# Two transformer blocks on one core: the first modulation as vector pieces, squares and means added on VectorE, activation tables loaded ahead

## What is computed

```python
# first block, layer 0 (mixer: latent attention, 8 heads), layer 1 (gated linear attention)
m_lat = (silu_c @ ada_w[i] + ada_b[i])      # 6 x 1024 values; m_ctx with silu_cc
h = modulate(rms_norm(x, norm_g[i, 0]), m[0], m[1])
x = x + m[2] * rms_norm(mixer(h), norm_g[i, 1])
h = modulate(rms_norm(x, norm_g[i, 2]), m[3], m[4])
x = x + m[5] * rms_norm(sqrelu_mlp(h, w1, w2), norm_g[i, 3])
# latent attention: s = q_nope.k_nope + q_rope.k_rope ; p = softmax(s * scale) ; o = p @ v
# second block: e = silu(c @ cond_w + cond_b); gated delta net, then retention, each followed by
# x = layer_norm(ALPHA * x + (1 + g) * y) and conv_ffn, modulated by e @ ada_w_2[i] + ada_b_2[i]
```

## Time and profile before

| | us |
|---|---|
| median of 3 runs | 3994.95 |
| lowest and highest run | 3993.47, 3996.55 |
| span of the profiled execution | 3992.8 |
| PE busy | 3715.2 (93%) |
| PE weight loads busy (beside PE) | 2882.0 |
| DVE busy | 1798.0 (45%) |
| ACT busy | 1229.2 (31%) |
| POOL busy | 156.4 |

### The profile page before, as it was taken

One profiled execution on the slowest core, in us unless ns is written; L12 is line 12 of the kernel. 1 busy time (PEld: TensorE's weight loads), 2 busy tenths in 40 slices (PEclk: granted clock), 3 DMA queues, 4 the chain that ended last, 5 costly groups with the idle time before them and its releaser, 6 DMA issues.

```text
span 3992.8 us, 45573 instructions
## 1 busy us (share of the span) xinstructions
PE 3715.2 (93%) x17382; PEld 2882.0 (72%) x17382; DVE 1798.0 (45%) x2588; ACT 1229.2 (31%) x1511; POOL 156.4 (4%) x292
## 2 busy tenths in 40 slices
PE   7899997999997999889998999979999999899998
PEld 3577786999994666668873666658877777768876
DVE  2244445454453333264444555647753344434433
ACT  3111125232223322253333333344432322334432
POOL 0000000010000000011110000002110000000000
PEclk9999998999998999999998999989999999999999
DMA  4111112333230110134441100015542222222222
GB/s 159 54 64 64 66 51 67 100 119 104 94 111 17 46 38 32 53 130 162 158 139 51 43 32 32 22 55 188 188 136 88 73 68 73 63 74 94 95 84 74
DMA packets 300087, 335.13 MB, mean 84 GB/s; under 512 B 12113, under 2 KB 266449, under 8 KB 299857
## 3 DMA queue, kind: packets, MB, share of 16 engines
q1 hardware_dynamic: 275408, 254.03, 19.7%
q0 software_dynamic: 23040, 75.52, 5.7%
q10 hardware_dynamic: 1537, 4.13, 0.3%
HBM read 331.55 MB, written 2.10 MB: 84 GB/s over the span
## 4 chain that ended last, share of the span: by engine, by line
PE 88%; DVE 4%; ACT 4%; issue 2%; DMA 2%; ACTq 0%; DVEq 0%; SPq 0%
PE acc L654 63%; PE sc L654 6%; PE sc L1118 2%; PE acc L850 1%; PE sc L685 1%; PE sc L824 1%; PE sc L826 1%; PE sc L688 1%; PE sc L762 1%; PE acc L1118 1%; PE acc L1289 1%; PE sc L695 1%; DMA wring<-in_mlp_w 1%; PE acc L993 1%; DVE arena L1767 1%
## 5 line engine op out<-in xcount | busy, mean ns | idle before, releaser
L654 PE MATMUL acc<-x_lo,w_hi 128*128 128x512 f32 (+1 forms) x2048 | 776.1, 379 | 35.5 <-DVE d_out_lo L1943 10.5
L1964 DVE TENSOR_TENSOR w_lo<-wring,w_hi 128x1024 fp32r<-128x1024 f32 (+1 forms) x368 | 412.6, 1162 | 571.9 <-ACT w_hi L1444 571.8
L1444 ACT ACTIVATE w_hi<-wring 128x1024 fp32r<-128x1024 f32 (+1 forms) x368 | 352.3, 1005 | 968.2 <-DMA wring<-in_mlp_w 479.1
L654 PEld LDWEIGHTS acc<-x_lo,w_hi 128*128 128x128 f32 x2048 | 389.1, 190 | 98.3 <-DVE w_lo L1964 28.4
L654 PE MATMUL acc<-hid_hi,w_hi 128*128 128x512 f32 (+1 forms) x1120 | 411.7, 368 | 7.8 <-DVE w_lo L1964 6.1
L654 PE MATMUL acc<-hid_hi,w_lo 128*128 128x512 f32 (+1 forms) x1120 | 409.0, 365 | 0.0
L654 PE MATMUL acc<-x_hi_holes,w_hi 128*128 128x512 f32 x704 | 280.3, 398 | 15.8 <-DVE x_lo L1970 15.1
L654 PE MATMUL acc<-x_hi_holes,w_lo 128*128 128x512 f32 x704 | 278.3, 395 | 0.0
L654 PE MATMUL acc<-hid_lo,w_hi 128*128 128x384 f32 (+1 forms) x768 | 270.8, 353 | 0.0
L654 PE MATMUL acc<-x_hi_seq,w_hi 128*128 128x512 f32 x576 | 228.9, 397 | 14.6 <-DVE x_lo L1973 14.6
L654 PE MATMUL sc<-hT,wring 128*128 128x512 f32 x512 | 237.6, 611 | 0.4 <-DVE d_col L2144 0.4
(11 more groups left out here) (384 smaller groups left out, 5968.5 us busy)
## 6 DMA issues: line engine op xcount, KB each, us to landing
wring<-in_mlp_w SPq DMA_DIRECT2D x64, 1024.0 KB, 5.5
rows_or_mod<-in_ada_w POOLq DMA_DIRECT2D x176, 256.0 KB, 3.2
wring<-in_ffn_up SPq DMA_DIRECT2D x44, 1024.0 KB, 5.0
wring<-in_ada_w SPq DMA_DIRECT2D x12, 2048.0 KB, 7.9
wring<-in_ret_w_in SPq DMA_DIRECT2D x24, 1024.0 KB, 5.3
rstd<-in_ada_w POOLq DMA_DIRECT2D x88, 256.0 KB, 3.4
wring<-in_ffn_down SPq DMA_DIRECT2D x32, 704.0 KB, 4.6
wring<-in_gdn_w_in SPq DMA_DIRECT2D x16, 1024.0 KB, 5.7
```

What stands on the lines that cost most here:

```text
L654: ins = pe.matmul(o, lhsT, rhs, start=start, stop=stop)
L1444: f(w_hi[s][:, c], wring[s][:, c], ACT.Copy).then_inc(w_high, 1)
L1964: tt(w_lo[s][:, c], wring[s][:, c], w_hi[s][:, c].bitcast(F32), SUB).then_inc(w_split, 1)
```

## The change

- `mla_pair` has 2 weight groups instead of 6. Chunks 2 to 5 of layer 0's modulation become pieces like those of the later layers: 32 between the copies of `mla_in` (`between`), 8 per iteration of `mla_pair` (`in_attention`), and 4 per iteration for the conditioning vector; POOL loads them into four slots, `first_sum` sums them on PE.
- The two rotary parts of a pair of heads lie side by side in the loaded weights (four DMAs instead of one) and are one product.
- Scores run two tiles ahead. The copy of the transposed tile and the product with the reciprocal move from DVE to ACT.
- `functions(name)` loads a named activation table set at chosen places; Ln and Exp share one set.
- For the norms y0, y1, y0m and y1m DVE adds the squares of seven blocks (`add_square`), and PE sums two buffers (`added_sum`). For the means of block two DVE adds seven blocks and PE sums two.
- The first two units of `mla_out`, `gla_out`, `gdn_out` and of each MLP quarter take turns over the input blocks (`turns`); the first unit of the FFN up stages and of `ret_head` takes its two halves in turn for each block.

```diff
-    ("mla_in", 1, 2, 6), ("mla_rope", 1, 0, 2), ("mla_pair", 4, 6, 34), ("mla_out", 1, 4, 8),
+    ("mla_in", 1, 2, 6), ("mla_rope", 1, 0, 2), ("mla_pair", 4, 2, 34), ("mla_out", 1, 4, 8),
...
+FIRST_BETWEEN = (5, 5, 6, 6, 5, 5)
...
+            pool.wait_ge(x_in, 32)
+            for p in range(FIRST_PIECES):
+                i, k = divmod(p, DB)
+                pool.wait_ge(mod_used[p % FIRST_SLOTS], first_piece(p))
+                pool.dma_start(first_w[p % FIRST_SLOTS],
+                               w[:, k, 2 * D + i * MOD_N:2 * D + (i + 1) * MOD_N]).then_inc(mod_loaded[p % FIRST_SLOTS], 16)
...
+            def added_sum(name, n):
+                _, b0, nb = NORMS[name]
+                for i, (done, count) in enumerate(((n_used, b0 + nb - 1), (n_sq, b0 + nb))):
+                    pe.wait_ge(done, count)
...
+            def mean_sum(stage, i):
+                pe.wait_ge(x_added, i + 1)
+                pe.matmul(sc[:, 0, 1, :], ones, sq[:, 0, 0:SEQ], start=True, stop=False)
+                emptied(pe, stage, *divmod(DB - 1, UNITS[stage]))
+                pe.matmul(sc[:, 0, 1, :], ones, xT[:, DB - 1, CTX:T], start=False, stop=True).then_inc(n_mean, 1)
...
+            def first_sum(done, i, column):
+                pe.wait_ge(mod_used[(DB - 1) % FIRST_SLOTS], done)
+                for m in range(MOD_N // P):
+                    for v in range(2):
+                        last = pe.matmul(column(2 * m + v), first_acc[:, i % 2, v, m * P:(m + 1) * P], ones[:, 0:1],
+                                         start=True, stop=True)
...
-                    if n < 8:
-                        if n % 4 == 0:
-                            columns[0] = group(S, it, 2 + n // 4, DB, 512)
-                        modulation(columns[0], n % 4, unit(S, 11 + 2 * n)[:, 1, 0:2], lambda k: cs[:, k, 0:2])
...
+                scores(1)
                 for n in range(2 * QT):
-                    if n + 1 < 2 * QT:
-                        scores(n + 1)
+                    turn(n)
+                    if n == 9:
+                        first_sum(...)
+                    if n + 2 < 2 * QT:
+                        scores(n + 2)
                     weigh(n)
...
+            def turns(nk):
+                together = [(v, k) for k in range(nk - 2) for v in range(2)]
+                return together + [(v, k) for v in range(2) for k in range(nk - 2, nk)]
...
+                    for v in range(2):
+                        claim(pe, S, it, v)
+                    for v, k in turns(DB):
+                        if v == 0:
+                            input_split(k, DB * i)
...
+            def functions(name):
+                act.preload_act_table_set(name)
...
+                    if name in ADDED:
+                        act.wait_ge(n_used, b0 + (b if b != 1 else 0))
...
+                functions(SILU)
                 with act.Fori(0, HIDB // 2 - 1) as it:
                     pair(it, False)
                 pair(HIDB // 2 - 1, True)
+                functions(LN_EXP)
...
+            def add_square(name, b, n):
+                _, b0, _ = NORMS[name]
+                dve.wait_ge(n_sq, b0 + b + 1)
+                if b > 1:
+                    dve.wait_ge(n_used, b0 + b)
+                tt(sq[:, 0, 0:n], sq[:, 0, 0:n], sq[:, 1, 0:n], ADD).then_inc(n_used, 1 if b > 1 else 2)
...
                             free(ins, S, u)
+                            if last and u >= 10:
+                                add_square(f"y{i}m", u - 9, n)
                         if 2 * u < MOD_PIECES[i]:
                             mod_piece(i, it, 2 * u + 1, ((0, 1), (2,))[i])
...
                 for j in range(8):
+                        if j >= 2:
+                            emptied(dve, stage, 0, j - 1)
+                            st.settle()
+                            ins = tt(total, xT[:, 0, CTX:T] if j == 2 else total, xT[:, j - 1, CTX:T], ADD)
```

More of the change, by code:

```diff
@@ L747, in _, with first_chunk @@
             last.then_inc(ada_done, 1)
[L749 to L753, removed]
+            def first_sum(done, i, column):
[4 more added lines that the diff above has]
+                                         start=True, stop=True)
+                last.then_inc(first_summed, 1)
+            def first_chunk(i):
+                first_sum(first_piece(i * DB + DB - 1) + 1, i, lambda c: mod_psum[:, MOD_AT + 32 + 8 * i + c:MOD_AT + 33 + 8 * i + c])
             def mod_sum(phase, it, i, nv):
@@ L893, in out_proj @@
                 if squares:
-                    square_sum(*squares, range(5, 8))
+                    added_sum(*squares)
             out_proj("mla_out", DB, 2, ("y0", T))
@@ L1486, in mlp @@
                 quarter(3, True)
-            emptied(act, "mla_pair", MLA_H // 2 - 1, 33)
-            for k in range(DB):
-                last = f(cs[:, k, 2:3], cs[:, k, 2:3], ACT.Silu, bias=col("cond_b", k))
+            functions(SILU)
+            act.wait_ge(cond_moved, 1)
+            last = f(cs[:, :, 2], cs[:, :, 2], ACT.Silu)
             last.then_inc(e_ready, 1)
+            functions(LN_EXP)
             high_weights("mla_out", 0, 0)
@@ L1773, in residual @@
                         MUL, ADD).then_inc(x_ready, 1)
+            for s in range(FIRST_SLOTS):
+                dve.memset(first_w[s][:, 0:1], 0.0).then_inc(mod_used[s], 1)
             dve.memset(eps[:, 0:1], 1e-6).then_inc(relu_free, 1)
@@ L1855, in _ @@
             for j in range(5):
+                for p in range(sum(FIRST_BETWEEN[:j]), sum(FIRST_BETWEEN[:j + 1])):
+                    between(p)
                 finished(dve, "mla_in", 0, j)
                 free(cp(halves(cq[:, j, :] if j < 3 else ckv[:, j - 3, :]), unit("mla_in", j)[:, :, 0:HALF]), "mla_in", j)
+            for p in range(sum(FIRST_BETWEEN[:5]), FIRST_PIECES):
+                between(p)
             finished(dve, "mla_in", 0, 5)
```

304 lines of the change are left out of this document (220 added, 84 removed).

## The result

The changed kernel takes 3872.3 us (median of 4 runs, 3864.65 to 3876.92) against 3994.21 of the kernel before beside it: a ratio of 0.9692, 95% interval 0.9679 to 0.9706. The profiled execution has a span of 3872.2 us, 120.6 less than before. The forecast was 3876, with 118.9 taken off the span.

The account below looks back on a forecast made before the run. PE, busy 93% of 3992.8 us, bounds the kernel; attention loop -67.6, pieces +4.6, cond chain +0.5, tables -25.9 and +2.6, means -15.6, squares -4.6, turns -12.9 sum to -118.9, forecasting 3876 us, range 3842 to 3908.

Parts of the forecast that it names:

- 46.0, 1.5, 1.5, 2.2 and 1.7 for the clock: `mla_pair`, tiles per iteration: PE work, wait before first transposes, narrow tiles, last weighings, low clock; 52.7 us against 66.8.
- the 1.5 us at the narrow tiles: `mla_pair`: PE waits about 1.5 us per iteration where next scores are narrow, PE needing 2.9 against DVE's 4.3.
- the 1.7 for a low clock: `mla_pair`: 1.7 us per iteration added for PE's stand before its first transposes and the low clock just after.
- Rival 4: `mla_pair`: PE stands briefly in many tiles and its clock stays at 1.2 GHz; 4060 us in all, chance 0.03.
- rival 1: `mla_in`: modulation pieces arrive slower than DVE uses them, 2.5 us per piece; +16 us, 3892 in all, chance 0.09.
- Rival 2: Table loads: own loads still precede Ln and Exp, explicit ones come on top; 25.9 gain gone, 3905 us, chance 0.07.
- rival 3: Table loads: the Trainium skill's drain of about 1380 ns is real at each switch; 26 more, 3850 us, chance 0.05.
- The +2.6 of `functions(LN_EXP)`: Behind both FFNs: the table load before `layer_norm_out` delays the split PE waits for; +2.6 us for two.
- the trap: Last MLP quarters: DVE waits for squares behind ACT's last `high_weights`; PE stands 6 us in `mlp0`, 6.4 in `mlp1`, clock 2.
- the tail: Sum of squares behind each MLP's last product: 6.8 us shorter in `mlp0` (4.9 for 10.33, plus 1.3 table load), 5.2 in `mlp1`.
- the upper bound of its range: All squares edits, forecast -4.6 us: -12 without PE's stands in the MLPs, 0 if the slow clock lasts.
- the recorded sum: Turns: -4.9 `mlp0`, -2.2 `mlp1`, -2.2 and -3.2 FFNs, -2.7 `ret_head`, +2.5 early claims; stated as -12.9 us.

## Why the prediction was right, point by point

**Attention loop: mechanism right, size short by 10.** The merged rotary part is as forecast: from the start of the iteration to the first scores 25.3 us instead of 28.2, 2.9 for 2.8. The tiles took 49.9 (332.85 to 382.79) instead of the 52.7 of the step "46.0, 1.5, 1.5, 2.2 and 1.7 for the clock". PE's waits after the first scores are 1.25 before the first transposes and 0.16, 0.97 and 0.90 in the last tiles, 3.3 in all. The two terms that failed are the 1.5 us at the narrow tiles (the one wait there is 0.1) and the 1.7 for a low clock, of which 0.6 is left (the clock is 1.00 in this iteration, 0.95 in the first and 0.98 in the second). Rival 4 did not come, since PE hardly stands inside the loop; the run with one tile ahead shows a milder form of it, 0.90, and that with the copies on ACT the safety lay in the second set of scores and not in the amount of work.

**Pieces in `mla_in`: right, slightly cheaper.** All six copies waited for PE and DVE waited for no load in the stage, so rival 1 fell. PE took 67.3 us from its first to its last product instead of 65.3, as two sums of 1.84 lie inside. The stage as a whole took 1.0 less than before in one profile and 2.4 less in the other, where +0.7 was put.

**Tables: right in total, 24 for 23.3, looser by stages.** Rival 2 (own loads on top) fell with the 42 loads, and rival 3 (the drain) with the run that has no named sets. The +2.6 of `functions(LN_EXP)` is there, 1.35 at each FFN. The prediction left two Ln loads out here and counted them under the squares, 1.3 behind each MLP's sum; with them its figure is 25.9.

**Means: mechanism right, 12 to 13 for 15.6.** Centring starts where it was put. What the sum left out is the longer stand of PE before the sum of squares, with a low clock in some of them.

**Squares: the trap right, the tail over-sized.** Stand and slow matmuls are 8.9 in `mlp0` (8 forecast), from the quarter's start to its last product. The step that failed is the tail in `mlp0`, where the added sum would start Ln at 4.9 behind the last product: it was 6.6, with the sum at the lower clock. The stand of 1.92 before the sum doesn't decide that by itself, since it is there with early squares too, at 2.85 for the sum; yet in all other kernels with this sum it takes 4.1 to 4.5 us, so the short one is the exception. The other part of the step is the 1.3 of the table load, in both MLPs, which is not the squares'. So in `mlp0` the edit cost 5.8 and not 1.2. With `mlp1` between 0 and 3 and the 9.1 of y0 and y1, whose stages came out as forecast, it is worth 0 to 3 us, where -4.6 was put (-2.0 without the two loads): near the upper bound of its range.

**Turns: 7 to 11 for 12.9, with a term too small.** At the turns between quarters 2.5 us were put, 0.5 each in `mlp0` and 0.3 in `mlp1`. From the last product of a quarter to the same product of the next they cost 1.4 in all in `mlp0` against the kernel before, as forecast, but 1.1 each in `mlp1`, 3.3. Whether that is the claim or the order of the blocks stays open. The gain at the start of `mlp0` was 4.4 for 4.9. (The terms of the recorded sum add up to 12.7, not 12.9.)

**Not in the sum: late weights in `mlp1`.** PE's waits for accumulators, most at units 10 and 14, add up to 6.1 us in the first profile and to between 4.3 and 7.6 in all eleven other profiles that have the change, against 1.7 in the kernel before and 1.6 in the same with scores two ahead. Of the miss of 6.2 there this is most, and the turns above are the next. It was not foreseen. No turns, squares back on PE, means back on PE, no named sets, copies on DVE and one set of scores each leave it standing, so none of these alone is its cause; no run names it.

**Not in the sum: the clock in stages that nobody changed.** The 6.2 of `gdn` instead of 1.3 is two iterations of `gdn_pair` of 113.1 us instead of 116.5. In the kernel before with scores two ahead, `gdn` took 507.3 instead of 510.35 with no edit there. At the same place of the second iteration, some 28 us from its start, the table of before has

```profile
2298.00:2302.00 4.00, 4.00 (x6) 1.49 (x5) 3.40 (x9) 3.99 (x5) 0.00 (x0) 0.50 0.00 0
```

and that of the changed kernel

```profile
2208.00:2212.00 4.00, 4.00 (x17) 2.29 (x16) 4.00 (x7) 3.97 (x5) 0.00 (x0) 1.00 0.00 0
```

PE is fully busy in both; before, the clock was at 0.50 of full speed, its lower level of 1.2 GHz. PE's last work before both rows is the same: four matmuls (eight records) that read 8 partitions instead of 128. Before, the last two of these records already take 1.06 us instead of 0.59; in the changed kernel all but the first take 0.59.

## What to carry to other kernels

When work leaves an engine that was full, ask first what it was hiding: in this loop the removed products filled the time in which Exp and the copies ran. With the copies on ACT and one set of scores the loop took 36 us more than before, and the whole kernel took as long as the kernel before, for all its other gains. (Copies on DVE with one set of scores were not run.) An operation that waits for another engine holds all that is queued behind it, so where a wait is put into a loop's last pass, read what stands before its signal on the engine that gives it; here moving four squares up was worth 15 us, some 2 of them by luck of the clock. Compare stages, not totals: the total was right within 4 us while single stages missed by 10.

## What the runs showed that was not expected

- The same code takes different times with the granted clock. `gla_gate` and `gla_head`, the same in ten of these kernels, took from 373.8 to 384.2 us, at clocks of 0.93 to 0.91; `gdn` took from 503.8 to 508.7. An edit that moves a stage's start can gain or lose 5 us in a later stage that it doesn't touch, so a term below that needs several kernels or its own rows.
- PE can fall to the lower clock while it counts as fully busy (0.50 at 2298 to 2302 above, with no idle time in the 14 us before it), here in matmuls that read only 8 partitions.
- The turn of a loop costs PE time that depends on more than its waits. With eight long fulfilled waits in unit 0 and no turns the first product of a quarter comes after 0.52 to 1.05 us of standing in `mlp0` and after none in `mlp1`; with the turns it is 1.09 and 0.83; with neither it is none.
